# Keys rotated on the TensorE beside their squares, PSUM reads put ahead of other steps in three loops

## The reference

```python
h = rmsnorm(x, norm_w[i])
proj = h @ w_in[i]
(u, s5_gate, z, xbc, dt_raw, q, k, v, att_gate, merge_logits) = jnp.split(proj, pts, axis=-1)
y_s5 = s5_mixer(u, ...) * jax.nn.silu(s5_gate)      # complex diagonal scan, GLU
y_ssd = ssd_mixer(z, xbc, dt_raw, ...)              # conv, softplus(dt), chunked scan, gated norm
y_att = window_attention(q, k, v, att_gate, ...)    # rmsnorm(q), rmsnorm(k), partial rotary, softmax
branches = jnp.einsum('blnw,nwd->blnd', ys, w_branch[i])
merged = jnp.sum(sigmoid(merge_logits) * branches, axis=2)
x = x + merged @ w_out[i]
```

## Time and profile before

| | |
|---|---|
| median of three executions | 1860.54 us (1859.03, 1860.54, 1862.31) |
| the profiled execution | 1864.92 us |
| its span, first to last instruction | 1863.2 us |
| TensorE busy | 1816.0 us (97%) |
| VectorE, ScalarE, GpSimd busy | 1376.3, 951.1, 547.2 us |
| mean granted TensorE clock | 0.997 of full |

### The profile page before, as it was taken

How to read it: one execution, slowest core, us unless ns; L and a number is a source line. 1 busy time by engine, 2 the same in 40 slices (tenths; PEclk the granted TensorE clock), 3 DMA queues, 4 the chain that set the end, 5 groups by cost and what they waited for, 6 DMA issues and landing times.

```text
span 1863.2 us, 35017 instructions
## 1 busy us (share of the span) xinstructions
PE 1816.0 (97%) x11720; PEld 1554.9 (83%) x11720; DVE 1376.3 (74%) x1867; ACT 951.1 (51%) x1128; POOL 547.2 (29%) x632
## 2 busy tenths in 40 slices
PE   5999999999999999999999999999999999999998
PEld 5898888877877898888899888887877778878887
DVE  6986666788787777666678766678787876766657
ACT  5334444656666564334354344446656575633334
POOL 5044444172452010002402433433452700000043
PEclk9999999999999999999999999999999999999999
DMA  7465555666455557665555555556465555566655
GB/s 288 142 207 193 195 179 200 193 204 212 164 206 202 177 177 267 228 229 210 217 189 178 188 194 180 201 206 204 171 209 201 193 186 182 192 247 240 235 203 204
DMA packets 80788, 377.00 MB, mean 202 GB/s; under 512 B 20848, under 2 KB 27536, under 8 KB 41872
## 3 DMA queue, kind: packets, MB, share of 16 engines
q1 hardware_dynamic: 76560, 360.00, 55.7%
q0 software_dynamic: 2368, 10.99, 1.5%
q10 hardware_dynamic: 1760, 4.75, 0.6%
HBM read 356.00 MB, written 21.79 MB: 203 GB/s over the span
## 4 chain that ended last, share of the span: by engine, by line
PE 84%; DVE 7%; issue 4%; DMA 2%; ACT 2%; POOL 1%; SPq 0%; DVEq 0%; ACTq 0%; POOLq 0%
PE mm L1705 21%; PE mm L1752 14%; PE mm L1753 13%; PE mm L1754 13%; PE mm L1709 11%; DVE w_lo L1036 2%; DMA raw<-in_stream 2%; PE mm L1695 1%; PE bs L1874 1%; PE mm L1697 1%; PE mm L1696 1%; PE b L1864 1%; PE bs L1880 1%; ACT w_hi L717 1%; PE b L1931 1%
## 5 line engine op out<-in xcount | busy, mean ns | idle before, releaser
L1036 DVE TENSOR_TENSOR w_lo<-raw,w_hi 128x2048 fp32r<-128x2048 f32 x299 | 697.4, 2337 | 237.0 <-ACT w_hi L717 227.8
L717 ACT ACTIVATE w_hi<-raw 128x2048 fp32r<-128x2048 f32 x299 | 569.9, 1912 | 428.9 <-DMA raw<-in_stream 425.7
L1705 PE MATMUL mm<-h_both,w_hi 128*128 128x512 f32 x1728 | 414.8, 392 | 0.0
L1705 PEld LDWEIGHTS mm<-h_both,w_hi 128*128 128x128 f32 x1728 | 317.4, 188 | 63.5 <-issue 0.3
L1752 PE MATMUL mm<-w_lo,h_both 128*128 128x512 f32 x768 | 306.8, 399 | 2.3 <-ACT gt L854 2.3
L1753 PE MATMUL mm<-w_hi,h_both 128*128 128x512 f32 x768 | 299.6, 390 | 0.0
L1754 PE MATMUL mm<-w_hi,h_both 128*128 128x512 f32 x768 | 299.4, 390 | 0.0
L1709 PEld LDWEIGHTS mm<-h_both,w_lo 128*128 128x128 f32 x1728 | 221.5, 191 | 8.4
L1709 PE MATMUL mm<-h_both,w_lo 128*128 128x256 f32 x1728 | 224.1, 283 | 0.0
L698 POOL TENSOR_TENSOR ssum<-ssum,proj 128x256 f32<-128x256 f32 x32 | 76.5, 2392 | 379.3 <-ACT proj L1005 352.6
L1752 PEld LDWEIGHTS mm<-w_lo,h_both 128*128 128x128 f32 x768 | 144.2, 188 | 37.5 <-ACT gt L854 6.7
(11 more groups left out here) (341 smaller groups left out, 2653.5 us busy)
## 6 DMA issues: line engine op xcount, KB each, us to landing
raw<-in_stream SPq DMA_DIRECT2D x300, 1024.0 KB, 4.9
gscr<-gt SPq DMA_DIRECT2D x48, 256.0 KB, 6.0
gin<-gscr SPq DMA_DIRECT2D x24, 512.0 KB, 5.7
bd<-in_bdense SPq DMA_DIRECT2D x16, 384.0 KB, 5.2
lam<-lscr SPq DMA_DIRECT2D x128, 32.0 KB, 3.4
crow<-cscr POOLq DMA_DIRECT2D x16, 256.0 KB, 5.5
x_old<-out POOLq DMA_DIRECT2D x2, 2048.0 KB, 12.5
out<-proj ACTq DMA_DIRECT2D x8, 512.0 KB, 5.3
```

The lines of the kernel that those rows point to most:

```text
L717: e.activation(w_hi[:, j % RAW, :], raw[:, j % RAW, :], ACT.Copy).then_inc(hi_done, 1)
L1036: e.tensor_tensor(w_lo[:, j % RAW, :], raw[:, j % RAW, :], w_hi[:, j % RAW, :].bitcast(F32), ALU.subtract).then_inc(lo_done, 1)
L1705: e.matmul(mm[:, j % 2, :], w_hi[:, j % RAW, k * P:k * P + P], h_both[:, k].rearrange("p a t -> p (a t)"), start=k == 0, stop=False)
```

## The change

1. **dt and `lam_T` later.** TensorE's `dt` and `lam_T` both come after pair 7 (before: after 6 and after 5). VectorE's `dt_x`, `dt_abs` go to step 7, ahead of `lo`; ScalarE's `lam_t`, `dt_exp` to step 8.
2. **Keys.** `k_norm` is multiplied into the rotation matrix (`rotk`, step 6), and TensorE rotates the raw keys right behind the squares, after pair 8 (before: after 13). `kn` falls away; the root is multiplied in at the end (step 14).
3. **The keys' root a slot on.** ScalarE's `inv_sqrt` "k" stands in step 10, behind `hi` of slot 13; VectorE's Newton step is cut in two, in steps 11 and 12.
4. **`dt_softplus` in four pieces** in steps 10, 11 and 12; `rotw` in step 14.
5. **Mixing:** `gate(g, 1)` ahead of the queries' root; `states` behind `st_make`.
6. **GLU:** `glu_t` ahead of `hi`.
7. **Branches:** `branch(n, 0)` ahead of `lo(2n + 3)`; in the last group the second `lo` behind `merge_lo`.

```diff
@@ -186,6 +186,7 @@
         rotw = sb("rotw", [P, P])
+        rotk = sb("rotk", [P, P])
         work = top[0]
@@ -776,7 +777,9 @@
             LA.mark(e.activation(sp[:, 6, :], sp[:, 4, :], ACT.Sin, scale=-TWO_PI / 2, bias=C("half_pi")), "s5_cos")
-        if n == 7:
+        if n == 8:
+            W.wait(LP, "lam_T")
+            LA.mark(e.activation(bw[:, 0, :], b5[:, 0:256], ACT.Copy), "lam_t")
             W.wait(LV, "dt_abs")
@@ -787,8 +790,6 @@
         if n == 6:
-            W.wait(LP, "lam_T")
-            LA.mark(e.activation(bw[:, 0, :], b5[:, 0:256], ACT.Copy), "lam_t")
             W.wait(LV, "k_raw")
@@ -797,7 +798,7 @@
             LA.mark(e.activation(bt[:, t % 2, :], kk[:, 2, 0:TOK] if t % 2 == 0 else kk[:, 2, TOK:], ACT.Tanh, scale=0.5), f"bc_tanh{t}")
-        if n == 9:
+        if n == 10:
             inv_sqrt(LA, "k", kk[:, 0, :], kk[:, 1, :], kk[:, 3, :], lambda: W.wait(LV, "k_v"))
@@ -892,14 +893,13 @@
                     gate(s // QUAD, 0)
-                if t == 1:
-                    inv_sqrt(MA, "q", qh[:], rq[:], rv[:], lambda: W.wait(MV, "q_v"))
                 if t == 5:
...
                 if t == 1:
+                    inv_sqrt(MA, "q", qh[:], rq[:], rv[:], lambda: W.wait(MV, "q_v"))
                     decay_exp()
@@ -949,6 +949,15 @@
             part(n, nb[0] + (n + 3), nj + n, t5)
+        else:
+            j = n - 8
+            e.wait_ge(pair_done, nb[0] + (n + 3))
+            if j >= 2:
+                W.wait(LV, f"glu_y{j - 2}")
+            for a in range(2):
+                m = 2 * j + a
+                LA.mark(e.activation(tg[:, j % 2, a, :], mm[:, n % 2, a * 256:a * 256 + 256], ACT.Tanh, scale=0.25,
+                                     bias=bgh[:, m:m + 1]), f"glu_t{m}")
         hi(nb, n + LEAD)
@@ -965,14 +974,6 @@
         if n >= 8:
-            j = n - 8
-            e.wait_ge(pair_done, nb[0] + (n + 3))
-            if j >= 2:
-                W.wait(LV, f"glu_y{j - 2}")
-            for a in range(2):
-                m = 2 * j + a
-                LA.mark(e.activation(tg[:, j % 2, a, :], mm[:, n % 2, a * 256:a * 256 + 256], ACT.Tanh, scale=0.25,
-                                     bias=bgh[:, m:m + 1]), f"glu_t{m}")
             if j < 3:
@@ -1044,11 +1045,19 @@

+    newton_product(S, nm, y, t, v)
+    newton_step(S, nm, y, t)
+
+def newton_product(S, nm, y, t, v):
+
     W.wait(S_A[S], nm + "_r")
...
     W.wait(S, nm + "_n2")
+
+def newton_step(S, nm, y, t):
+
     S.mark(e.tensor_scalar(t, t, -0.5, 1.5, ALU.mult, ALU.add), nm + "_n3")
@@ -1195,16 +1204,23 @@

-    def dt_softplus():
+    def dt_ratio():

...
         chain(tt_(D(4), D(3), D(3), ALU.mult))
-        chain(e.tensor_scalar(D(5), D(4), 1.0 / 17, None, ALU.mult))
-        for k in (15, 13, 11, 9, 7, 5, 3):
+
+    def dt_series(part):
+
+        if part == 0:
+            chain(e.tensor_scalar(D(5), D(4), 1.0 / 17, None, ALU.mult))
+        for k in ((15, 13, 11, 9), (7, 5, 3))[part]:
             chain(e.scalar_tensor_tensor(D(5), D(5), 1.0 / k, D(4), ALU.add, ALU.mult))
+
+    def dt_steps():
+
         chain(e.scalar_tensor_tensor(D(5), D(5), 1.0, D(3), ALU.add, ALU.mult))
@@ -1267,6 +1283,13 @@
             LV.mark(ins, "dt_s")
+        if n == 7:
+            W.wait(LP, "dt")
+            for t in range(2):
+                LV.mark(tt_(sd[:, 0, t * 16:t * 16 + 16], b6[:, 256 + t * 16:272 + t * 16], PR("dt_bias", 0, 16), ALU.add),
+                        f"dt_x{t}")
+            W.wait(LV, "dt_x1")
+            chain(e.scalar_tensor_tensor(D(1), D(0), -1.0, D(0), ALU.mult, ALU.max), "dt_abs")
         if n:
@@ -1280,13 +1303,6 @@
             c_gamma(n - 8)
-        if n == 6:
-            W.wait(LP, "dt")
-            for t in range(2):
-                LV.mark(tt_(sd[:, 0, t * 16:t * 16 + 16], b6[:, 256 + t * 16:272 + t * 16], PR("dt_bias", 0, 16), ALU.add),
-                        f"dt_x{t}")
-            W.wait(LV, "dt_x1")
-            chain(e.scalar_tensor_tensor(D(1), D(0), -1.0, D(0), ALU.mult, ALU.max), "dt_abs")
         if 6 <= n < 10:
@@ -1297,14 +1313,19 @@
             conv(bc_dst(t), proj[:, BC + t, :], lambda k, t=t: PR("conv", (8 + t) * 5 + k), LV, f"bc_conv{t}_")
+        if n == 11:
+            dt_series(0)
         if n == 12:
-            dt_softplus()
+            newton_step(LV, "k", kk[:, 0, :], kk[:, 1, :])
+            dt_series(1)
+            dt_steps()
         if n == 9:
...
         if n == 10:
-            newton(LV, "k", kk[:, 0, :], kk[:, 1, :], kk[:, 3, :])
-            chain(e.scalar_tensor_tensor(kk[:, 1, :], ktf, PR("k_norm"), kk[:, 0, :], ALU.mult, ALU.mult), "kn")
+            dt_ratio()
+        if n == 11:
+            newton_product(LV, "k", kk[:, 0, :], kk[:, 1, :], kk[:, 3, :])
         if n == 13:
@@ -1314,14 +1335,18 @@
                 LV.mark(e.scalar_tensor_tensor(gm[:, g, 256:384], b[:, 256:384], 0.25, tri, ALU.mult, ALU.mult), f"gm{g}2")
-        if n == 11:
+        if n == 6:
+            chain(e.tensor_scalar(rotk[:], C("rot"), PR("k_norm"), None, ALU.mult), "rotk")
+        if n == 14:
             chain(e.tensor_scalar(rotw[:], C("rot"), PR("q_norm"), None, ALU.mult), "rotw")
-        if n == 14:
-
-            LV.mark(tt_(two(kk[:, 0, :]), two(kk[:, 1, :]), twice(C("cos")), ALU.mult), "k_c")
+        if n == 13:
+            chain(e.scalar_tensor_tensor(two(kk[:, 1, :]), two(ktf), PR("k_norm"), twice(C("cos")), ALU.mult, ALU.mult), "k_c")
             W.wait(LP, "k_rot")
             chain(tt_(two(kk[:, 3, :]), two(b6[:]), twice(C("sin")), ALU.mult))
-            chain(tt_(ktf, kk[:, 0, :], kk[:, 3, :], ALU.add), "k_fin")
+        if n == 14:
+
+            chain(tt_(kk[:, 1, :], kk[:, 1, :], kk[:, 3, :], ALU.add))
+            chain(tt_(ktf, kk[:, 1, :], kk[:, 0, :], ALU.mult), "k_fin")
             chain(e.tensor_scalar(small[:, 9:10], C("half_pi"), 0.0, None, ALU.mult), "prep_end")
@@ -1500,11 +1525,12 @@
                         forth()
-                        states()
                     newton(MV, "q", qh[:], rq[:], rv[:])
...
                     st_make()
+                    if c:
+                        states()
                     lo(nb, s + LEAD)
@@ -1632,14 +1658,17 @@
     for n in range(N_GROUP):
+        branch(n, 0)
         lo(nb, 2 * n + LEAD)
-        branch(n, 0)
         branch(n, 1)
...
             glu_lo(3)
-        lo(nb, 2 * n + 1 + LEAD)
+        if n < N_GROUP - 1:
+            lo(nb, 2 * n + 1 + LEAD)
         if n % 3 == 2:
             merge_lo(n // 3)
+        if n == N_GROUP - 1:
+            lo(nb, 2 * n + 1 + LEAD)

@@ -1807,14 +1836,13 @@
             LP.mark(ins, "dt_t")
-        if n == 6:
+        if n == 7:

...
             LP.mark(ins, "dt")
-        if n == 5:
             W.wait(LV, "powers")
@@ -1822,7 +1850,10 @@
             W.wait(LA, "k_sq")
+            W.wait(LV, "rotk")
+            W.wait(LV, "dt_x1")
             LP.mark(e.matmul(b7[:], C("blk"), kk[:, 0, :], start=True, stop=True), "k_ss")
+            LP.mark(e.matmul(b6[:], rotk[:], kt[:].rearrange("p a b -> p (a b)"), start=True, stop=True), "k_rot")
         if n == 15:
@@ -1837,9 +1868,6 @@
                 LP.mark(e.matmul(b[:, 256:384], proj[:, BC + g, P:TOK], proj[:, BC + 2 + g, P:TOK], start=True, stop=True), f"G{g}")
-        if n == 13:
-            W.wait(LV, "kn")
-            LP.mark(e.matmul(b6[:], C("rot"), kk[:, 1, :], start=True, stop=True), "k_rot")
```

## The result

The changed kernel takes **1841.9 us** (median of four executions, 1841.65 to 1841.99) against 1861.34 us of the kernel before (four executions, 1859.03 to 1862.31): a ratio of 0.9899, 95% interval 0.9887 to 0.9912. A second series gave 1841.69 us (1841.38 to 1841.89) against 1859.28 (1857.17 to 1862.39, nine executions), 0.9906 (0.9891 to 0.9921). The forecast was 1840.0 in a range of 1834 to 1850. The profiled executions can be laid beside each other: 1841.99 us and a span of 1840.2, against 1864.92 and 1863.2. The span fell by 23.0 us; the sum of the prediction was 23.7.

What follows compares the result with a forecast made beforehand. TensorE, busy 97% of the span, was taken as the bound, leaving only its waits and low clock to win. Terms 4.1 + 4.7 + 3.4 + 4.1 + 2.9 + 4.5 = 23.7 us gave 1840 us, range 1834 to 1850.

Steps and rivals of the forecast that it cites:

- `lam_T`: Preparation, both layers: issued two slots later, TensorE's `lam_T` no longer waits for `rtok`; gain 4.1 us.
- GLU: Last GLU pair: with `glu_t` ahead of the rounding, TensorE's waits for it go; gain 4.1 us.
- branches: Branch blocks: `acc` no longer stands behind `lo`, so TensorE's waits for bank reads go; gain 2.9 us.
- The clock: Preparation: two falls of TensorE's clock to the lower level vanish with the stalls before them; gain 3.4 us.
- The preparation's bank reads: VectorE's late bank reads, four waits: root behind the rounding and softplus spread over three steps; gain 4.7 us.
- The rule weighed against the change: VectorE and GpSimd lock a shared port pair; short softplus steps could each wait, making the bank-read term about 2.8 us.
- Mixing: Mixing blocks: second gate read moved ahead of the queries' root removes eight waits of 0.56 us; gain 4.5 us.
- A: Whole kernel: the sum of the terms holds, time within 1835 to 1844 us; chance 0.62.
- B: Preparation: VectorE stays too late, bank-read and clock gains lost or halved; 1845 us, to 1849 if `k_ss` waits; chance 0.18.
- C: GLU and branches: loads are the real cause, so 4.1 + 2.9 us are given back; 1847 us; chance 0.11.
- D: Mixing: slower, because the queries' root waits for the bank read and `qh` comes late; chance 0.05.
- E: Whole kernel: nothing measurable, each stall returns at the next place; 1857 to 1861 us; chance 0.04.

## Why the prediction was right, point by point

- **What bounds the kernel** held. So did, roughly, the price of a wait as idle time and about 0.27 us: the eight gate reads (2.4 idle, 4.6 paid) show it best. The addition is not one number: 0.16 us at pair 15, as the prediction's own 1.89 lost for 1.73 idle says, 0.29 at gates and branches when undone, 0.3 at the GLU.
- **`lam_T`, GLU, branches**: 4.1, 4.1 and 2.9 predicted, 4.3, 4.2 and 3.0 found between starts of the two traces. Nothing is late in their place.
- **The clock**: both falls are gone, worth 3.2 us for 3.4. The second was sized as 5 us x (1 - 0.66), but TensorE was busy for only 4.44 of these 5 us, and by the starts it cost 1.5. The waits of 0.8 us that remain pulled nothing down.
- **The preparation's bank reads are the step that failed**: 4.7 predicted, 3.2 measured. Two of the prediction's own signs say so: the line on `proj` is 1.6 us and not under 1, and pair 15 waits for VectorE. The reason of the term was right (the root ahead of the rounding; undoing it brought back 3.90 us of idleness). The spare of 0.6 us at pair 15 was not there. Two things in my laying-out were too kind. I let all 3.9 idle us come back, and 2.3 came, since the next rounding stands behind the root in turn. And I kept the softplus at its old 8.2 us, "since the old softplus has these waits in its 8.2 us already". Cut into pieces it meets other instructions of GpSimd: the part in step 12 takes 5.2 us where it takes 1.7 with GpSimd elsewhere.
- **The rule weighed against the change** was the one to follow. The traces agree with it: VectorE's step of 1.15 us ends within 0.03 us of GpSimd's instruction, and takes 0.18 without it. By the Trainium skill, SBUF — State Buffer, section "SBUF: two separate sides", the term would have been about 2.8; 3.2 came. I had the row of 1.16 us and set the rule aside.
- **Mixing**: 4.5 predicted, 5.0 found, because a gate's wait slows the steps for some 2.5 us behind it and costs 0.62 and not 0.56. But "`states` itself: nothing" was wrong: it is worth 2.3 us, being what makes room for the gate's gain. The sum held because both moves were in the change; that is luck as far as the reason goes.
- **The program's start** differs by 0.36 us between the profiles; this was in no term, and is the run's, not the change's.
- **The translation to a median.** I took 1840.0, between 1836.8 and 1840.2, because the medians' clock was unknown. From the profiled execution alone the sum gave 1841.2, and its like measured 1841.99. The changed kernel hardly scatters (0.3 us in four executions, where the kernel before has 3.3), so there is little between its profiled execution and its median, and the profile's sum was the better guide.
- **Rivals.** A happened. B, VectorE too late, happened in a small part: two waits that cost 1.9 us with their restarts, far from its 1845, since the clock held. (B's 1845 is worked out from 1836.8 and C's 1847 from 1840; from one base they would differ by about a us.) C (loads), D (the queries' root) and E (the stalls return) did not: no wait on a load, `qh` a full us early, and a time that followed the idle time.

## What to carry to other kernels

When an engine's read of a bank is late, look for the first place where that engine is idle, and at what stands in front of the step that it waits for: here one root ahead of a rounding was worth over 8 us together with the stalls and clock falls that it caused. Lay VectorE's short steps out with the durations that they will have beside GpSimd's instructions at the new place, and keep the last of them behind the bank read. Two moves that meet at one engine must be costed together: the gate's read alone would have been worth about half.

## What the runs showed that I had not expected

- A VectorE step on 32 numbers a partition takes 0.18 us alone and 1.15 us beside a GpSimd instruction of 1.35 us; the 512-wide product of the Newton step in step 12 takes 1.05 us beside GpSimd and 0.69 without it. It goes the other way too: in the changed kernel a copy by GpSimd that started 0.1 us behind a 2048-wide `w_lo` (118.33, 2.27 us) took 2.63 us, and the next like it 0.61:

```profile
118.44 2.63 POOL L599 COPY cz<-cl 64x512 f32<-64x512 f32 x1 [0.17 <-POOL cur L590]
121.25 0.61 POOL L599 COPY cz<-cl 64x512 f32<-64x512 f32 x1 [0.17 <-POOL cz L599]
```

- The size of a stall alone does not tell whether the clock falls. With the softplus whole, an idle time of 2.69 us at pair 15 of the first layer was followed by full clock, and one of 2.0 us in the second layer by 0.71. In the kernel before, 2.28 us and 1.89 us were followed by a fall, and 1.73 us at pair 15 and 1.99 us at the GLU were not. So a remaining stall of about 2 us costs its length, or its length and some 1.5 us. That this is also why the executions of the kernel before scatter (over 3.3 us, the changed one's over 0.3) is likely and not shown. The mean clocks of its timed executions point that way in two series of nine: 0.999 for the fastest (1857.17 and 1856.54 us), 0.997 for the slowest (1862.39 and 1861.07). In a third series they are not ordered.
